# Three group norms share one root and one reciprocal, and an expert's first weight parts get a fourth home

## What is computed

```python
h = rmsnorm(x, norm_mix_g)
pu, rx, rgate, q, kv, ng, sc = split_cols(h @ w_in, SPLIT_SIZES)
y_pool, y_rg, y_nsa, y_sc = pool_mixer(...), rglru_mixer(...), nsa_attention(...), short_conv(...)
og = mix_out_g.reshape(4, 256)
y = concat([rmsnorm(yi, og[i]) for i, yi in enumerate((y_pool, y_rg, y_nsa, y_sc))])
x = x + y @ w_out
x = x + moe_ffn(rmsnorm(x, norm_ffn_g), ...)      # 4 groups of 8 experts, top group, top 2 in it

def rmsnorm(x, g):
    return x * rsqrt(mean(x * x) + 1e-6) * g
def expert(xi, e):                                # w_gu[e] is 1024 x 1024, w_down[e] is 512 x 1024
    a, b = split(xi @ w_gu[e], 2)
    return (silu(a) * b) @ w_down[e]
```

## Time and profile before

| | |
|---|---|
| median of three runs | 842.99 us (842.6 to 844.31) |
| the profiled execution's own time | 844.27 us |
| its span, first to last instruction | 842.5 us |
| TensorE busy | 720.6 us (86%) |
| VectorE / ScalarE / GpSimd busy | 203.0 / 152.2 / 182.4 us |
| DMA queue of SyncE | 230.96 MB, 69.3% of 16 engines' span |
| chain that ended last, by engine | TensorE 42%, SyncE's queue 37%, DMA 9%, VectorE 5% |

### The profile page before, as it was taken

How to read it: one execution, slowest core, us unless ns; L and a number is a source line. 1 busy time by engine, 2 the same in 40 slices (tenths; PEclk the granted TensorE clock), 3 DMA queues, 4 the chain that set the end, 5 groups by cost and what they waited for, 6 DMA issues and landing times.

```text
span 842.5 us, 10234 instructions
## 1 busy us (share of the span) xinstructions
PE 720.6 (86%) x3647; PEld 373.2 (44%) x3647; DVE 203.0 (24%) x575; ACT 152.2 (18%) x363; POOL 182.4 (22%) x188
## 2 busy tenths in 40 slices
PE   6999999999988999499999997877777877877883
PEld 6788788778666446333333322222222222222220
DVE  2421305628495114710110101001001001001020
ACT  5223423033635211110000000000000000000000
POOL 5010000333000000123243241322232232232221
PEclk9999999999989999699999999999999999999998
DMA  9652942021700993499999999999999999999992
GB/s 302 123 152 69 280 159 59 1 77 34 268 1 5 391 420 140 160 348 414 408 408 417 402 406 412 418 408 414 413 408 412 416 409 412 415 414 410 415 413 73
DMA packets 76885, 246.52 MB, mean 293 GB/s; under 512 B 24944, under 2 KB 44303, under 8 KB 52235
## 3 DMA queue, kind: packets, MB, share of 16 engines
q1 hardware_dynamic: 63697, 230.96, 69.3%
q0 software_dynamic: 11776, 8.58, 4.6%
q10 hardware_dynamic: 1378, 6.54, 1.9%
HBM read 239.95 MB, written 24.92 MB: 314 GB/s over the span
## 4 chain that ended last, share of the span: by engine, by line
PE 42%; SPq 37%; DMA 9%; DVE 5%; issue 3%; ACT 2%; POOL 1%; ACTq 0%; POOLq 0%; DVEq 0%
PE bank L1111 40%; SPq L588 25%; SPq L595 11%; DMA reg_a<-in_exp_w_gu 3%; DMA reg_b<-in_exp_w_gu 3%; PE bank L1114 2%; DMA ffn_in<-reg_x 1%; DMA reg_x<-in_x_prompt 1%; DVE reg_a L1897 1%; DVE reg_y L2107 1%; DVE reg_b L1672 1%; DVE small L1857 1%; ACT reg_y L1094 0%; DVE reg_y L1904 0%; POOL small L693 0%
## 5 line engine op out<-in xcount | busy, mean ns | idle before, releaser
L1111 PE MATMUL bank<-reg_w,reg_y 128*64 128x512 f32 (+2 forms) x512 | 136.8, 572 | 15.7 <-DMA reg_w<-in_exp_w_gu 15.7
L1111 PE MATMUL bank<-reg_a,reg_y 128*64 128x512 f32 x528 | 122.8, 600 | 22.7 <-DMA reg_a<-in_exp_w_gu 17.0
L1111 PE MATMUL bank<-reg_b,reg_y 128*64 128x512 f32 x528 | 122.9, 600 | 21.4 <-DMA reg_b<-in_exp_w_gu 15.8
L2111 DVE TENSOR_TENSOR reg_y<-reg_y,bank 128x256 f32<-128x256 f32 x32 | 13.5, 421 | 417.1 <-ACT reg_y L1094 417.1
L1111 PEld LDWEIGHTS bank<-reg_w,reg_y 128*64 128x64 f32 (+2 forms) x512 | 45.3, 144 | 95.2 <-issue 54.1
L1111 PE MATMUL bank<-reg_b,reg_w 128*128 128x260 f32 x384 | 85.6, 383 | 0.0
L1111 PEld LDWEIGHTS bank<-reg_a,reg_y 128*64 128x64 f32 x528 | 34.3, 137 | 102.5 <-issue 49.4
L1111 PEld LDWEIGHTS bank<-reg_b,reg_y 128*64 128x64 f32 x528 | 34.6, 136 | 100.7 <-issue 57.8
L1111 PEld LDWEIGHTS bank<-reg_b,reg_w 128*128 128x128 f32 x384 | 72.6, 190 | 11.9 <-issue 1.0
L1114 PE MATMUL bank<-small,reg_y 128*128 128x128 f32 (+3 forms) x206 | 42.7, 317 | 24.6 <-DVE reg_y L2111 15.0
L1094 ACT ACTIVATE reg_y<-bank,small 128x256 f32<-128x256 f32 x32 | 15.2, 474 | 262.0 <-PE bank L1111 262.0
(11 more groups left out here) (357 smaller groups left out, 641.0 us busy)
## 6 DMA issues: line engine op xcount, KB each, us to landing
reg_a<-in_exp_w_gu SPq DMA_DIRECT2D x44, 1024.0 KB, 27.8
reg_b<-in_exp_w_gu SPq DMA_DIRECT2D x44, 1024.0 KB, 27.7
reg_w<-in_exp_w_gu SPq DMA_DIRECT2D x40, 1024.0 KB, 27.8
reg_a<-in_exp_w_down SPq DMA_DIRECT2D x22, 1024.0 KB, 28.1
reg_b<-in_exp_w_down SPq DMA_DIRECT2D x22, 1024.0 KB, 28.0
reg_h<-in_exp_w_down SPq DMA_DIRECT2D x20, 1024.0 KB, 27.8
reg_w<-in_w_in SPq DMA_DIRECT2D x9, 1024.0 KB, 10.7
reg_w<-in_w_out SPq DMA_DIRECT2D x2, 2048.0 KB, 11.0
```

Source lines behind the costliest of these rows:

```text
L1111: return eng.matmul(out, lhsT, rhs, start=start, stop=stop, skip_group_check=True)
L2111: tt(hid[b], silu[b], bank[2 + b][:, 256:512], ALU.mult).then_inc(S["hid_made"], 1)
```

## The change

The sums of the three groups go to 32 partitions each of one bank: the weights are 32 columns of `ones`, and group g writes to partitions 32g to 32g + 31. One root and one reciprocal of 96 x 512 (and x 8) then serve all three groups. As VectorE now needs the factor on all 128 partitions, TensorE spreads row 32g of the reciprocals with a selecting matrix (`group_sel`, made in step 5 from the identity) in steps 11, 12 and 13 (jobs NB0 to NB2, and NBs), and VectorE multiplies out of PSUM, in the same three steps. `yT_ready` comes in step 13 in place of 12.

`x_in` becomes a fourth home for parts 0 and 1 of gate and up. These parts of expert e are in home e % 4, and are asked for one expert earlier than before. The other parts and the down halves stay in home e % 3. Parts 0 and 1 of expert 3 are loaded between those of expert 2, as soon as the tiles whose memory they take are squared and stored twice. One semaphore for each tile (`x_moved`) counts its load and its two stores. TensorE's code is 12 experts in a loop and 8 after it, SyncE's 1, 12 in a loop and 4.

```diff
...
@@ psum_jobs @@
         if step == NORM_STEP:
-            for g in range(3):
-                take(f"N{g}")
+            take("N")
             take("Ns")
+        if NORM_STEP + 3 <= step < NORM_STEP + 6:
+            take(f"NB{step - NORM_STEP - 3}")
+            if step == NORM_STEP + 3:
+                take("NBs")
...
@@ memory @@
+        gu_first = [[w[:, 0:2, :], w[:, 2:4, :]] for w in gu_w]
+        gu_first.append([x_in[:, 0:2, :], x_in[:, 2:5:2, :]])
+        group_sel = p_masked[0:96, 0:384].rearrange("p (g n) -> p g n", g=3)
+        roots = reg_a.t[0:96, 5200:5200 + T]
...
@@ SyncE @@
+            def load_expert(e, j, first):
+
+                if j < N_EXP - 2:
+                    load_gu(e + 1, (j + 1) % 4, (0, 1), first + e - 2)
+                if j == N_EXP - 1:
+                    load_gu(e, j % 4, (0, 1), first + e - 3)
+                load_gu(e, j % 3, (2, 3), first + e - 2)
+                load_down(e, j % 3, first + e - 2)
...
-                with eng.Fori(1, N_EXP // 3) as i:
-                    for g in range(3):
-                        e = 3 * i + g
-                        load_gu(e, g, first + e - 2)
-                        load_down(e, g, first + e - 2)
-                for e in range(N_EXP - N_EXP % 3, N_EXP):
-                    load_gu(e, e % 3, first + e - 2)
-                    load_down(e, e % 3, first + e - 2)
+                load_expert(3, 3, first)
+                with eng.Fori(0, 2) as i:
+                    for j in range(4, 16):
+                        load_expert(12 * i + j, j, first)
+                for e in range(28, N_EXP):
+                    load_expert(e, e, first)
...
             eng.wait_ge(bank_full[bank_of["Y3.0"]], turn_of["Y3.0"] + 1)
-            load_gu(2, 2, parts=(0, 1))
+            load_gu(2, 2, (0, 1))
+            for part, tiles in ((0, (0, 1)), (1, (4, 2))):
+                eng.wait_ge(S["x1_ss"], 8 + part)
+                for i in tiles:
+                    eng.wait_ge(x_moved[i], 16 * 3)
+                load_gu(3, 3, (part,))
             eng.wait_ge(bank_full[bank_of["Y3.1"]], turn_of["Y3.1"] + 1)
-            load_gu(2, 2, parts=(2, 3))
+            load_gu(2, 2, (2, 3))
...
@@ GpSimd @@
-            eng.wait_ge(S["ffn_in_stored"], 16 * NTILE)
-            eng.wait_ge(S["x1_stored"], 16 * NTILE)
+            for i in range(NTILE):
+                eng.wait_ge(x_moved[i], 16 * 3)
...
@@ ScalarE, step 8 @@
-                    for g in range(3):
-                        ps = taken(eng, f"N{g}")
-                        copied(eng.activation(m[4 + g // 2][:, g % 2, 0:SEQ], ps[:, :], ACT.Sqrt, scale=1.0 / GW, bias=eps_col), f"N{g}")
+                    ps = taken(eng, "N")
+                    copied(eng.activation(roots[:, 0:SEQ], ps[0:96, :], ACT.Sqrt, scale=1.0 / GW, bias=eps_col[0:96]), "N")
                     ps = taken(eng, "Ns")
-                    eng.activation(m[4][:, :, SEQ:T], ps[:, 0:16].rearrange("p (j t) -> p j t", j=2), ACT.Sqrt, scale=1.0 / GW, bias=eps_col)
-                    copied(eng.activation(m[5][:, 0, SEQ:T], ps[:, 16:24], ACT.Sqrt, scale=1.0 / GW, bias=eps_col), "Ns")
+                    copied(eng.activation(roots[:, SEQ:T], ps[0:96, 0:NS], ACT.Sqrt, scale=1.0 / GW, bias=eps_col[0:96]), "Ns")
...
@@ TensorE @@
-                    for g in range(3):
-                        eng.wait_ge(S["sq_made"], g + 1)
-                        ps = claim(eng, f"N{g}")
+                    eng.wait_ge(S["sq_made"], 3)
+                    for name, lo, hi in (("N", 0, SEQ), ("Ns", SEQ, T)):
+                        ps = claim(eng, name)
                         for j in range(2):
-                            ins = mm(ps[:, :], ones, m[g][:, j, 0:SEQ], j == 0, j == 1)
-                        filled(ins, f"N{g}")
-                    ps = claim(eng, "Ns")
-                    for g in range(3):
-                        for j in range(2):
-                            ins = mm(ps[:, 8 * g:8 * g + 8], ones, m[g][:, j, SEQ:T], j == 0, j == 1)
-                    filled(ins, "Ns")
+                            for g in range(3):
+                                ins = mm(ps[32 * g:32 * g + 32, 0:hi - lo], ones[:, 0:32], m[g][:, j, lo:hi], j == 0, j == 1)
+                        filled(ins, name)
+                if NORM_STEP + 3 <= step < NORM_STEP + 6:
+
+                    g = step - NORM_STEP - 3
+                    eng.wait_ge(S["nrm_made"], 1)
+                    filled(mm(claim(eng, f"NB{g}")[:, :], group_sel[:, g, :], roots[:, 0:SEQ], True, True), f"NB{g}")
+                    if g == 0:
+                        ps = claim(eng, "NBs")
+                        for x in range(3):
+                            ins = mm(ps[:, 8 * x:8 * x + 8], group_sel[:, x, :], roots[:, SEQ:T], True, True)
+                        filled(ins, "NBs")
...
@@ VectorE @@
-                    rs = m[4 + g // 2][:, g % 2, :]
-                    eng.reciprocal(rs, rs).then_inc(S["nrm_made"], 1)
-                if step == NORM_STEP + 4:
-                    eng.wait_ge(S["nrm_made"], 3)
-                    for g, first in ((0, 0), (1, 2), (2, 6)):
-                        rs = m[4 + g // 2][:, g % 2, :]
-                        for j in range(2):
-                            gain = params[:, P_OUT_G + first + j:P_OUT_G + first + j + 1]
-                            ins = stt(yT[:, first + j, :], yT[:, first + j, :], gain, rs, ALU.mult, ALU.mult)
-                    ins.then_inc(S["yT_ready"], 1)
+                if step == NORM_STEP - 3:
+                    eng.tensor_copy(group_sel, ident[0:96, 0:96:32].unsqueeze(2).to_broadcast([96, 3, 128]))
+                if step == NORM_STEP + 1:
+                    drained(eng, "N")
+                    drained(eng, "Ns")
+                    eng.reciprocal(roots, roots).then_inc(S["nrm_made"], 1)
+                if NORM_STEP + 3 <= step < NORM_STEP + 6:
+                    g = step - NORM_STEP - 3
+                    firsts = (0, 2, 6)
+                    if g == 0:
+                        ps = taken(eng, "NBs")
+                        for x in range(3):
+                            for j in range(2):
+                                at = firsts[x] + j
+                                ins = stt(yT[:, at, SEQ:T], yT[:, at, SEQ:T], params[:, P_OUT_G + at:P_OUT_G + at + 1], ps[:, 8 * x:8 * x + 8], ALU.mult, ALU.mult)
+                        copied(ins, "NBs")
+                    ps = taken(eng, f"NB{g}")
+                    for j in range(2):
+                        at = firsts[g] + j
+                        ins = stt(yT[:, at, 0:SEQ], yT[:, at, 0:SEQ], params[:, P_OUT_G + at:P_OUT_G + at + 1], ps[:, :], ALU.mult, ALU.mult)
+                    copied(ins, f"NB{g}")
...
```

More of the change, by code:

```diff
@@ L587, in load_gu @@
                     src = gu_dram[bass.ds(e, 1)].rearrange("e p s c n -> (e p) s c n")[:, lo // 4, lo % 4:lo % 4 + width, :]
-                    eng.dma_start(gu_w[g][:, lo:lo + width, :], src).then_inc(gu_loaded[g][part], 16)
+                    home = gu_first[g][part] if part < 2 else gu_w[g][:, lo:lo + width, :]
+                    eng.dma_start(home, src).then_inc(gu_loaded[g][part], 16)
             def load_down(e, g, free=None):
@@ L767, in _ @@
                 eng.wait_ge(S["idx_made"], r + 1)
-                eng.sem_inc(S["scatter_asked"], 1)
+                eng.sem_inc(S["passed"], 1)
                 gather(0)
@@ L1525, in _, with expert @@
             rounds = eng.value_load(n_rounds[0:1, 0:1], min_val=1, max_val=ROUNDS)
-            def expert(n, b, g, loads, gathered):
+            def expert(n, b, g, loads, first, first_loads, gathered):
                 eng.wait_ge(S["xe_made"], n + 1)
@@ L1533, in expert @@
                     if within == 0:
-                        eng.wait_ge(gu_loaded[g][part], loads)
+                        eng.wait_ge(gu_loaded[first if part < 2 else g][part], first_loads if part < 2 else loads)
                     for s in range(2):
-                        w = gu_w[g][:, c, :].rearrange("p (h f) -> p h f", h=2)[:, :, 256 * s:256 * s + 256]
+                        w = (gu_first[first][part][:, within] if part < 2 else gu_w[g][:, c]).rearrange("p (h f) -> p h f", h=2)[:, :, 256 * s:256 * s + 256]
                         ins = mm(bank[2 + b][64 * s:64 * s + 64, :].rearrange("p (h f) -> p h f", h=2), xe[b][:, c % 4, c // 4, :], w, c == 0, c == KC - 1)
@@ L1558, in _ @@
                 gate_table()
[L1559 to L1560 removed]
+                with eng.Fori(0, 2) as i:
+                    for j in range(12):
                         g = j % 3
[L1562 to L1563 removed]
+                        expert(N_EXP * r + 12 * i + j, j % 2, g, 16 * USES[g] * r + 64 * i + 16 * (j // 3) + 16, j % 4, 128 * r + 48 * i + 16 * (j // 4) + 16, 256 * r + 96 * i + 16 * ((j + 1) // 2) + 16)
+                for e in range(24, N_EXP):
                     g = e % 3
```

50 lines of the change are left out of this document (23 added, 27 removed).

## The result

The changed kernel takes 839.82 us (median of 7 runs, 834.88 to 842.26), the kernel before it, run beside it, 844.35 (842.6 to 845.74): a ratio of 0.9934, 95% interval 0.9913 to 0.9955. It is faster by 4.5 us, where 9.4 were forecast. The profiled execution took 836.96 us, with a span of 835.2 against 842.5. One execution of the kernel before, beside the third group of experiments, took 1477 us and is left out of every ratio and range.

A forecast was written before the change was run, and what follows sets the result against it. The prediction took a full DMA queue in the expert stage as the bound; attention 4.3 plus fourth home 5.1 gave 9.4 us, so 833.6 us against a median of 842.99, range 831.5 to 837.5.

The forecast's parts named there:

- The loads' place: Routing: expert 3's two early loads fit idle DMA stretches, part 1 asked for at about 336; added wait put at nothing.
- The second rival: Early loads collide with the last tile's store, making it 2.5 us later: 836.1 us in all; chance 0.10.
- The fourth home: Expert stage: two of 172 weight parts leave the full DMA queue, saving 5.1 us, or 5.4 at the other end.
- burst: Attention loop, TensorE: the 24 records of the sums fall from 6.61 to 2.5 us.
- second table load: Attention loop, ScalarE: the load back to exponentials comes at 224.6 in place of 228.48, 3.9 us earlier.
- maxima of step 11: Attention loop, VectorE: row maxima start at about 234.9 in place of 242.23, 7.3 us ahead.
- TensorE's wait for NB0's bank: Attention loop: NB1 must wait until VectorE has read the bank it shares with NB0; TensorE idles some 2.5 us.
- scores of step 14: Attention loop, TensorE: these start at about 248.0 in place of 252.63, 4.6 us ahead.
- attention shorter, full clock: Attention loop: the change to the norms saves 5.0 us if TensorE's clock stays at full level.
- The clock: Attention loop: TensorE's new idle may lower its clock, costing 0 to 3 us; taken as 0.7, leaving 4.3 us gained.
- Everything up to 359.50 moves by 4.3: All work until expert 0 has used its first part comes 4.3 us earlier, as the attention does.
- the third rival: TensorE's clock stays low in the attention loop: attention gives 2.3 us, total 7.4, time 835.6 us; chance 0.14.

The follow-up runs named there:

- the home alone: Only the new place for expert 3's first two weight parts, norms as before, against the kernel before: 841.13 us, ratio 0.9966.
- norms alone: Only the change to the norms, weight stream as before, against the kernel before: 841.49 us, ratio 0.9975.

## Why the prediction was right or wrong

**What bounds the kernel: right.** The expert stage is a full DMA queue before and after (share 1.02 from 440 to 820 us), and what isn't loaded in it shortens it.

**The loads' place: right.** Part 1 was asked for at about 333, the store took 8.84 us, the gather 3.00. The second rival didn't come in the changed kernel; one profile of the home alone had a store of 10.65.

**The fourth home: 5.1 forecast, 3.9 measured, and both my ends (5.1 and 5.4) above it.** This is the first step that failed. I priced the two parts by their bytes alone and left the price of the other 170 as it was. The change also split eight of them into smaller packets, and had TensorE fetch code in the full stage eight times and not three. I saw both in the diff, the slice with the step of two and the loop of 12, and asked of the second only whether TensorE would stall. The pieces account for 0.3 to 0.5 of the missing 1.2 us; the fetches may be the rest, by one profile. In a stage whose bound is the DMA queue, the question for every edit is what it adds to the queue.

**The norms' steps: right nearly throughout.** On the scale of before (the rows of after plus the 3.0 of the early start):

| step | forecast | after |
|---|---|---|
| burst | 2.5 long | 2.02 |
| second table load | 224.6 | 224.4 |
| maxima of step 11 | 234.9 | 234.9 |
| TensorE's wait for NB0's bank | 2.5 | 2.17 |
| scores of step 14, full clock (norms alone, 245.48 plus its 3.3) | 248.0 | 248.8 |
| attention shorter, full clock | 5.0 | 4.6 |

The column groups overlap better than I took: 6.61 to 2.02 is 3.3 times. The reciprocal on 96 partitions took the same 3.39 us, as forecast.

**The clock: the second step that failed.** I took 0.7 of a range of 0 to 3 as a sort of mean. The runs don't lie about a mean: of five profiles with that wait unfilled four fell, and the attention was 42.66 to 42.76, against 40.10 in the fifth. The likely value was 2.6, so this is the largest single miss, 1.9 us. The granted clock of 0.50 at 246 us, behind 3.06 us of idling, already showed a fall behind such a pause; it stood in the third rival, to which I gave 0.14.

**"Everything up to 359.50 moves by 4.3": the third.** It came 1.6 later in the profile, as the projection's 76 records took 10.67 us. I had read the earlier trace rows, the same records at full clock, and took the clock of that stage as given, a term put at nothing. It is the same mechanism one stage on. Together: 2.0 - 1.6 + 3.9 = 4.3, against the 9.4. The missing 5.1 us are 1.9 for the clock in the loop, 0.4 for the loop at full clock, 1.6 for the clock in the projection and 1.2 for the stream.

**The chances** for the sign were right. The range's upper end, 837.5, held the third rival alone, but neither a smaller fourth home nor a second fall. Part of the distance is not the change's: the forecast of 833.6 counts from a median of 842.99, and the kernel before took 844.35 beside the result. That is 1.4 of the 6.2 us between 833.6 and 839.8. And that the sum of one pair of profiles, 4.3, lies so near the 4.5 of the medians is in part luck, as the attention alone differs by 2.6 us from one execution to another.

## What to carry to other kernels

Before spreading results through banks handed out in turn, count the jobs between two of them, and look for a bank that is free over that stretch: here that, with the order of the steps around it, was worth 3.2 us, and 5.8 with the clock. Where TensorE pauses for two microseconds ahead of a stage that it bounds, look at the clock of that stage, in several profiles; an idle matmul there can be worth more than the work saved. Then look at the whole run again, as here a fall that was removed in one place was followed by others elsewhere. In a stage bound by a full DMA queue, count packets and code fetches beside the bytes.

## What the runs showed of the hardware

- The granted clock differs from one execution to the next behind the same pause: after 2.16 to 2.17 us, NB1 took 2.04 to 2.05 us in four profiles and 1.10 in one. In the changed kernel's expert stage six of twelve waits of 2.0 to 2.5 us had a fall behind them. Once it fell with no pause over 0.4 us. The Trainium skill ("TensorE: Matmul & The Clock Gate", "What's actually happening") says that the chip looks at the engine's activity in a window that runs freely, not in step with the kernel. By that the same pause can bring a fall in one execution and none in the next; the traces agree. The window itself no trace shows.
- A fall was free where VectorE was the bound (step 12 of before) and cost 1.4 to 4.8 us where TensorE was (76 records of 8.99 in 10.35 to 11.69; the loop's 40.10 in 42.66, and 36.87 in 41.64). Whether the scatter of the runs comes from it is not shown: of the kernels with the norms' half, three have a profile with no fall in the loop or the projection, and their runs lay 1.7 us (5 runs), 4.4 (6) and 10.7 (12) apart.
- Three column groups: 24 records, half of them 512 columns wide, in 2.02 us and not 6.61, 3.3 times faster. The Trainium skill ("TensorE: Matmul & The Clock Gate", "Measured speedup vs the span model") gives 2.38 for three groups of 512 columns. The trace's factor is higher, and the measurement decides here; it is not quite the same comparison, as half of the records have 8 columns and the weights went from 128 columns to 32.
- A destination in 4 KB pieces in place of 8 KB: 4.4 us for 7424 packets more in a full queue, 0.6 for each 1024.
- A fetch of 16 KB of TensorE's code in a full queue: 0.26 us, by one profile; the medians of the runs don't confirm it.
